# Weight panels of a transformer stack: a ring of two raw panels and four low parts becomes one ring of six, written in place

## What is computed

```python
for l in range(2):                          # D = 1024, SEQ = 256
    mod = silu(c) @ w_mod[l] + b_mod[l]     # [1, 6*D]: shift1, scale1, gate1, shift2, scale2, gate2
    h = rms_norm(x, norm1) * (1 + scale1) + shift1
    proj = h @ w_in                         # pooled part u, queries, keys/values of 3 branches, gates
    mix = concat([pool_mixer(u), nsa_mixer(q, k, v, gates)]) @ w_out
    x = x + gate1 * mix
    h2 = rms_norm(x, norm2) * (1 + scale2) + shift2
    x = x + gate2 * (square(relu(h2 @ w_ff1)) @ w_ff2)      # D_FF = 4096
# then one layer: projections, dilated attention, a two-way SSD scan, gated mix, layer norm,
# a feed-forward of width 4096, layer norm
```

## Time and profile before

| | before |
|---|---|
| median of 3 runs | 1370.56 us (1369.36 to 1371.61) |
| the profiled execution | 1369.93 us, its span 1368.1 us |
| TensorE matmul busy | 1270.2 us (93%) |
| VectorE busy | 937.6 us (69%) |
| ScalarE busy | 620.8 us (45%) |
| DMA moved | 247.69 MB, 49.7% of 16 engines' time on SyncE's queue |
| mean granted TensorE clock | 0.944 of full speed |

### The profile page before, as it was taken

The page is one execution under the profiler, slowest core; times in us unless marked ns, Lnnn a source line. Parts: engine busy times, 40 slices in busy tenths (PEclk is TensorE's granted clock), DMA queues, the critical chain, the costliest instruction groups (busy, mean ns, idle before and its releaser), DMA issues.

```text
span 1368.1 us, 21735 instructions
## 1 busy us (share of the span) xinstructions
PE 1270.2 (93%) x8834; PEld 1162.2 (85%) x8834; DVE 937.6 (69%) x1223; ACT 620.8 (45%) x828; POOL 38.4 (3%) x42
## 2 busy tenths in 40 slices
PE   6699999999998989899999998998889998999997
PEld 6587897999988779799998997886769987899996
DVE  5778868887875687775557559987865653755553
ACT  2444225444444522454444444468875532644432
POOL 1001200000000130000000000000000000000000
PEclk8699699999999989999999999999889999999999
DMA  9534554776744064465555642356744451555530
GB/s 381 214 132 154 185 199 165 281 285 242 283 155 154 31 243 156 166 216 184 184 184 215 208 154 99 120 197 205 231 159 143 155 177 60 185 196 185 186 140 31
DMA packets 43621, 247.69 MB, mean 181 GB/s; under 512 B 4160, under 2 KB 12368, under 8 KB 15520
## 3 DMA queue, kind: packets, MB, share of 16 engines
q1 hardware_dynamic: 43104, 244.57, 49.7%
q0 software_dynamic: 448, 2.14, 0.5%
HBM read 245.58 MB, written 1.11 MB: 180 GB/s over the span
## 4 chain that ended last, share of the span: by engine, by line
PE 69%; DVE 17%; DMA 6%; ACT 5%; issue 2%; SPq 0%; POOL 0%; DVEq 0%; ACTq 0%
PE bank L388 14%; PE bank L390 13%; PE bank L389 13%; PE bank L687 12%; PE bank L688 6%; DVE w_lo L383 4%; DMA arena<-in_modw 2%; DVE arena L1017 2%; ACT w_hi L378 2%; PE bank L809 2%; DVE arena L1916 1%; DVE macc L1017 1%; DMA arena<-dscr 1%; DMA raw<-in_panels 1%; PE bank L477 1%
## 5 line engine op out<-in xcount | busy, mean ns | idle before, releaser
L383 DVE TENSOR_TENSOR w_lo<-raw,w_hi 128x2048 fp32r<-128x2048 f32 x170 | 388.7, 2290 | 186.3 <-ACT w_hi L378 185.9
L378 ACT ACTIVATE w_hi<-raw 128x2048 fp32r<-128x2048 f32 x170 | 324.1, 1910 | 229.7 <-PE bank L390 117.3
L687 PE MATMUL bank<-act,w_hi 128*128 128x512 f32 x768 | 280.2, 406 | 12.3 <-DVE act L1038 5.5
L388 PE MATMUL bank<-act,w_hi 128*128 128x256 f32 x800 | 238.1, 298 | 8.6 <-DVE act L1038 7.2
L388 PE MATMUL bank<-ff_hi,w_hi 128*128 128x256 f32 (+1 forms) x816 | 230.3, 282 | 1.8 <-issue 1.0
L389 PE MATMUL bank<-act,w_hi 128*128 128x256 f32 x800 | 230.7, 288 | 0.0
L390 PE MATMUL bank<-ff_hi,w_lo 128*128 128x256 f32 (+1 forms) x816 | 230.7, 283 | 0.0
L389 PE MATMUL bank<-ff_lo,w_hi 128*128 128x256 f32 (+1 forms) x816 | 230.6, 283 | 0.0
L390 PE MATMUL bank<-act,w_lo 128*128 128x256 f32 x800 | 230.5, 288 | 0.0
L688 PE MATMUL bank<-act,w_lo 128*128 128x256 f32 x768 | 217.7, 283 | 0.0
L687 PEld LDWEIGHTS bank<-act,w_hi 128*128 128x128 f32 x768 | 146.1, 190 | 51.4 <-issue 10.9
(11 more groups left out here) (320 smaller groups left out, 1767.0 us busy)
## 6 DMA issues: line engine op xcount, KB each, us to landing
raw<-in_panels SPq DMA_DIRECT2D x170, 1024.0 KB, 4.9
arena<-in_modw SPq DMA_DIRECT2D x48, 1024.0 KB, 6.8
mixf<-dscr SPq DMA_DIRECT2D x8, 512.0 KB, 6.0
arena<-dscr SPq DMA_DIRECT2D x8, 512.0 KB, 4.9
mixf<-dscr SPq DMA_DIRECT2D x8, 256.0 KB, 6.3
arena<-dscr SPq DMA_DIRECT2D x8, 256.0 KB, 6.4
cst<-in_cst SPq DMA_DIRECT2D x1, 1251.5 KB, 7.6
arena<-in_x SPq DMA_DIRECT2D x1, 1024.0 KB, 5.0
```

The source lines that it names most:

```text
L378: nc.scalar.activation(w_hi[slot(k)][:, :], raw[:, k % RAW, :], ACT.Copy).then_inc(hi_done, 1)
L383: nc.vector.tensor_tensor(w_lo[slot(k)][:, :], raw[:, k % RAW, :], w_hi[slot(k)][:, :].bitcast(F32), ALU.subtract).then_inc(lo_done, 1)
L388: nc.tensor.matmul(o, wh, xh, start=start, stop=False, skip_group_check=skip)
L687: nc.tensor.matmul(bank[4 + c][:, :], wh[:, s:s + P], act2[:, kc, :, :], start=kc == 0, stop=False)
```

## The change

`raw` and `w_lo` become one ring of six panels. The low part overwrites the raw panel that it is made from. `load` of panel n waits until TensorE has used panel n-6; the first six loads wait for nothing. The memory is the same. The four high parts stay as they are, with their waits.

SyncE's order changes with it. Panels 2 to 5 are loaded at the start, and every later load stands earlier in the order in relation to the units and fetches around it: in the first two layers load 14 now stands ahead of unit 17, load 15 ahead of unit 18, load 16 ahead of unit 19, load 17 ahead of units 20 and 21. In the feed-forward of layer 0 each pass has load, unit, load, unit, load, load. In the third layer the list is load 22, 23, fetches, 24, 25, fetches, 26 and so on, as before, without the loops around it.

Since six slots and four panels in a pass don't divide, the loops of six passes become two passes with three bodies each, on SyncE, ScalarE, VectorE and TensorE.

```diff
-        raw = sb("raw", [P, RAW, PANEL])
+        with nc.sbuf_tensor("raw", [P, RING_W, PANEL], F32) as raw:
+            pass
+        ring_w = sb("ring_w", [P, RING_W, PANEL], F32R)
         w_hi = [sb(f"w_hi{i}", [P, PANEL], F32R) for i in range(SPLIT)]
-        w_lo = [sb(f"w_lo{i}", [P, PANEL], F32R) for i in range(SPLIT)]
...
+        def place(m, k):
+
+            return divmod(4 * (m.c if isinstance(m, Turn) else m) + k, RING_W)
...
+        def landed(eng, m, k):
+            n, at_slot = place(m, k)
+            eng.wait_ge(raw_ready[at_slot], 16 * (n + 1) + (32 * m.i if isinstance(m, Turn) else 0))
...
         def load(sp, m, k):
 
-            sp.wait_ge(lo_done, 4 * m + k - RAW + 1)
-            sp.dma_start(raw[:, k % RAW, :], a["panels"][4 * m + k]).then_inc(raw_ready[k % RAW], 16)
+            n, at_slot = place(m, k)
+            if n:
+                sp.wait_ge(split_free, SPLIT + 4 * m + k - RING_W + 1)
+            sp.dma_start(w_raw(m, k), a["panels"][4 * m + k]).then_inc(raw_ready[at_slot], 16)
...
             m = 11 * l
-            load(sp, m, 2)
-            load(sp, m, 3)
             if l == 0:
                 load_mod(sp, l, 8)
-            if l == 0:
                 load_mod(sp, l, 9)
-            for k in (4, 5, 6):
-                load(sp, m, k)
+            load(sp, m, 6)
+            load(sp, m, 7)
             if l == 0:
                 load_mod(sp, l, 10)
-            load(sp, m, 7)
             load(sp, m, 8)
+            load(sp, m, 9)
             if l == 0:
                 load_mod(sp, l, 11)
-            for k in (9, 10, 11):
-                load(sp, m, k)
+            load(sp, m, 10)
             load_mod(sp, l, 12)
+            load(sp, m, 11)
             load_mod(sp, l, 13)
+            load(sp, m, 12)
             load_mod(sp, l, 14)
-            load(sp, m, 12)
             load_mod(sp, l, 15)
             load(sp, m, 13)
-            for u in (16, 17, 18):
-                load_mod(sp, l, u)
+            load_mod(sp, l, 16)
             load(sp, m, 14)
+            load_mod(sp, l, 17)
+            load(sp, m, 15)
+            load_mod(sp, l, 18)
+            load(sp, m, 16)
             load_mod(sp, l, 19)
-            load(sp, m, 15)
+            load(sp, m, 17)
             load_mod(sp, l, 20)
             load_mod(sp, l, 21)
-            for k in (16, 17, 18):
+            for k in (18, 19, 20, 21):
                 load(sp, m, k)
-            with sp.Fori(1, FF_STEPS // 2 - 1) as i:
-                load(sp, m + i, 15)
...
+            with sp.Fori(0, FF_PASSES) as i:
+                for n in range(1, 4):
+                    mm = Turn(i, m + n)
+                    load(sp, mm, 18)
                     for mp in range(2):
-                        sp.wait_ge(mod_used, MOD_PANELS * l + 20 + 2 * i + mp + 1)
-                        sp.dma_start(modw[:, mp, :], a["modw"][MOD_PANELS * l + 20 + 2 * i + mp]).then_inc(modraw[mp], 16)
-                for k in (16, 17, 18):
-                    load(sp, m + i, k)
+                        if ahead:
+
+                            u = MOD_PANELS * l + 20 + 2 * n + mp + 6 * i
+                            sp.wait_ge(mod_used, u + 1)
+                            sp.dma_start(modw[:, mp, :], a["modw"][u]).then_inc(modraw[mp], 16)
+                        load(sp, mm, 19 + mp)
+                    load(sp, mm, 21)
             e = m + FF_STEPS // 2 - 1
-            load(sp, e, 15)
             for u in (34, 35) if ahead else (22, 23):
                 load_mod(sp, l, u)
-            load(sp, e, 16)
-            load(sp, e, 17)
+            for k in (18, 19, 20, 21):
+                load(sp, e, k)
...
             dve.wait_ge(hi_done, 4 * m + k + 1)
-            nc.vector.tensor_tensor(w_lo[slot(k)][:, :], raw[:, k % RAW, :], w_hi[slot(k)][:, :].bitcast(F32),
+            nc.vector.tensor_tensor(w_lo(m, k), w_raw(m, k), w_hi[slot(k)][:, :].bitcast(F32),
                                     ALU.subtract).then_inc(lo_done, 1)
...
+            for k in range(2, RING_W):
+                load(sp, 0, k)
             for l in range(layers):
                 sp_layer(sp, l, l + 1 < layers)
```

More of the change, by code:

```diff
@@ L176, in build @@
         act_ready = sem("act_ready")
-        raw_ready = [sem(f"raw_ready{i}") for i in range(RAW)]
+        raw_ready = [sem(f"raw_ready{i}") for i in range(RING_W)]
         hi_done = sem("hi_done")
@@ L296, in slot, with __init__, __rmul__, w_raw @@
             return k % SPLIT
+        class Turn:
+            def __init__(self, i, c):
+                self.i, self.c = i, c
+            def __rmul__(self, four):
+                return 3 * four * self.i + four * self.c
+        def place(m, k):
+            return divmod(4 * (m.c if isinstance(m, Turn) else m) + k, RING_W)
+        def w_raw(m, k):
+            return raw[:, place(m, k)[1], :]
+        def w_lo(m, k):
+            return ring_w[:, place(m, k)[1], :]
+        def landed(eng, m, k):
+            n, at_slot = place(m, k)
+            eng.wait_ge(raw_ready[at_slot], 16 * (n + 1) + (32 * m.i if isinstance(m, Turn) else 0))
         RING = "ADAD" + "DDAD" + "D" * 5 + "A" * 8 + "D" * 7 + "A" * 8
@@ L524, in cmp @@
                     s = slice(jj * P, (jj + 1) * P)
-                    last = mm3(bank[6][:, 0:60], w_hi[slot(L_CMP)][:, s], w_lo[slot(L_CMP)][:, s], tbh[:, jj, :], tbl[:, jj, :],
+                    last = mm3(bank[6][:, 0:60], w_hi[slot(L_CMP)][:, s], w_lo(m, L_CMP)[:, s], tbh[:, jj, :], tbl[:, jj, :],
                                jj == 0, jj == 15)
@@ L705, in pe_ff @@
                 pe_mod(pe, 12 * l + 10, macc, MOD_AT + 40)
[L706 to L712, removed]
+            with pe.Fori(0, FF_PASSES) as i:
+                for n in range(1, 4):
+                    mm, j = Turn(i, m + n), j0 + 2 * n + 6 * i
+                    up(mm, k0 + 1, j + 1, 1)
+                    down(mm, k0 + 2, j, 0, False, False)
+                    up(mm, k0 + 3, j + 2, 0)
+                    down(mm, k0 + 4, j + 1, 1, False, False)
+                    if mods == "ahead":
+                        pe_mod(pe, 12 * l + 10 + n + 3 * i, macc, MOD_AT + 40 + 4 * n + 12 * i)
             e = m + FF_STEPS // 2 - 1
@@ L991, in ff_schedule @@
             step(m, j0 + 1, k0 + 1, 1, None, (k0 + 5, k0 + 6), 1)
-            with eng.Fori(1, FF_STEPS // 2 - 1) as i:
-                step(m + i, j0 + 2 * i, k0 - 1, 0, k0 - 2, (k0 + 3, k0 + 4), i)
-                step(m + i, j0 + 2 * i + 1, k0 + 1, 1, k0, (k0 + 5, k0 + 6), i)
+            with eng.Fori(0, FF_PASSES) as i:
+                for n in range(1, 4):
+                    mm, j = Turn(i, m + n), j0 + 2 * n + 6 * i
+                    step(mm, j, k0 - 1, 0, k0 - 2, (k0 + 3, k0 + 4), 3 * i + n)
+                    step(mm, j + 1, k0 + 1, 1, k0, (k0 + 5, k0 + 6), 3 * i + n)
             e = m + FF_STEPS // 2 - 1
@@ L1413, in finish @@
         def finish(sp):
-            for k in range(2, 6):
+            for k in range(6, 22):
                 load(sp, M2, k)
-            with sp.Fori(0, 4) as i:
-                for k in (6, 7, 8, 9):
-                    load(sp, M2 + i, k)
             load(sp, M2, 22)
@@ L1438, in finish @@
                         fetch(sp, e)
-            with sp.Fori(7, 19) as i:
-                for k in (6, 7, 8, 9):
-                    load(sp, M2 + i, k)
+            for k in range(34, 82):
+                load(sp, M2, k)
             for half in range(2):
@@ L2098, in _ @@
                 if u in (5, 6):
-                    sp.dma_start(raw[:, u - 5, :], a["panels"][u - 5]).then_inc(raw_ready[u - 5], 16)
+                    load(sp, 0, u - 5)
+            for k in range(2, RING_W):
+                load(sp, 0, k)
             for l in range(layers):
```

20 lines of the change are left out of this document (10 added, 10 removed).

## The result

| | before | after |
|---|---|---|
| median of 4 runs each | 1369.96 us (1365.85 to 1371.61) | 1404.01 us (1400.38 to 1409.16) |
| the profiled execution | 1369.93 us | 1405.27 us, its span 1403.4 us |
| TensorE matmul busy | 1270.2 us | 1281.4 us |
| mean granted TensorE clock | 0.944 | 0.935 |

The ratio is 1.0256, 95% interval 1.0215 to 1.0297: slower by 34 us. The forecast was 1394.0 in a range up to 1404, so the direction was right, the size was short by 10 us, and the median lies just outside. Four more runs of the changed kernel, with a second profile, gave 1398.11 (1395.32 to 1404.27). Every run lists its mean granted clock, and the time goes with it: the two shortest of the eight (1395.32 and 1395.45 us) had 0.941, the longest (1409.16) 0.929.

The account below looks back on a forecast made before the run. TensorE's matmuls bound the kernel, busy 93% of the span, about 98 us idle. From 1369.93 us, gains of 14.2 and losses of 37.9 (21.4 + 8.4 + 6.3 + 1.8) gave 1393.6, stated as 1394, range 1380 to 1404.

Parts of the forecast that it names:

- the last units: Last w_mod units of the first two layers: late by 1 to 3 us, costing +0.6 and +1.2 us.
- End of the attention, +21.4: Layers 0 and 1: units 17 and 19, queued behind waiting loads, land late; +10.9 and +10.5 us, before clock loss.
- The clock: TensorE's clock drops after the holes before mod(4) and the sums: 1.8 + 2.4 us per layer, +8.4, between 0 and 12.
- unit 12: Layer 1: this unit is issued behind a load whose awaited panel is long released, winning 1.0 us.
- Feed-forward of layer 0, +6.9: One late unit costs 1.05 us in each of six passes, +6.3 (0 to 9); the layer's last units add +0.6.
- Gains, -14.2: Panel 2 gaps 8.8, unit 12 of layer 1 1.0, first down projection of layer 3 0.9, scan 3.5 us.
- The gaps at panel 2: First two layers: earlier panel 4 wins 1.7 us in layer 0, 4.7 plus 2.4 of clock in layer 1; sum -8.8.
- The scan: Loads leave right behind the previous fetches, shortening three waits in TensorE's path: -3.5 us, between 0 and -7.
- rival A: Faster: the units' late issue is hidden and only the earlier panels count, 1355.7 us; chance 0.04.
- Costs put at 0: Split in place costs nothing; longer loop bodies taken as 0, with up to 2 us for instruction fetch.
- Rival B: Slower by the two holes alone: no clock lost at them, loop absorbs its late unit, 1378.9 us; chance 0.13.
- Rival C: Slower still: loop loses 1.5 us a pass, clock 12, gains 9, longer bodies cost 2; 1407 us; chance 0.08.

Follow-up runs that it names:

- Experiments 1: Changed kernel with the w_mod units at the end of the attention of layers 0 and 1 again ahead of the loads: 1368.45 us, 0.9984 of before.
- 4: Kernel before, with SyncE waiting ahead of load 14, unit 18 and unit 19 until panels 8, 9 and 10 are used: 1407.31 us, 1.0266 of before.
- 5: Changed kernel with only unit 17 moved ahead of load 14 in the first two layers: 1389.48 us.
- 6: Changed kernel with only unit 19 moved ahead of load 16 in the first two layers: 1382.03 us.
- 9: Kernel before with only the feed-forward loops of the first two layers unrolled to two passes of three bodies: 1369.26 us, ratio 1.000.
- 10: Kernel before with 17 idle matmuls (2.0 us) ahead of the second half of panel 5 of layer 1: 1369.85 us.
- experiment 2: Changed kernel with feed-forward units issued a pass early, behind loads that have gone some 6 us earlier: 1392.34 us, 1.0162 of before.

## Why the prediction was right or wrong

**The mechanism** was right at each place where a loss was forecast: unit 17 behind panel 8, unit 19 behind panel 10, one unit in each loop pass, the last units. Experiments 1, 4, 5 and 6 show it from both sides.

**End of the attention, +21.4, with clock +29.8.** The traces have +33.0: TensorE is busy 10.5 us longer (8.4 forecast for the clock) and idle 22.5 longer (21.4). Unit 17 landed 8.7 us behind the release of panel 8, not 7.4, and a whole 8.32 behind its own issue, so TensorE stood 4.50 us before mod(4), not 3.2; unit 19 landed 7.3 behind panel 10, as said. The Trainium skill, DMA: Bandwidth & Descriptors, section Bandwidth, gives 6.15 us for 1 MB, measured on transfers issued from GpSimd. Here SyncE issues them, and the changed kernel's panels landed in 4.8 at the median and its units in 6.9, so the trace agrees with it for neither.

**The clock.** At the holes it was lost as forecast, if by 2 us more: low for 17.1 us in layer 0 and 13.7 and 20.5 in layer 1, never before. The step that failed is that it was looked for only there (8.4 us in the sum, 12 at the upper end) and put at nothing where the change brings no wait. In the attention of layer 1 the same work ran 5.3 and 10.0 us slower in the two profiles. In the eight profiles with the ring and no idle work, or with it ahead of panel 50, the stretch averages 50.2 us, 4.5 over before. Together with 1.0 for unit 12, 3.2 more at the holes, 1.7 more at the last units and in the third layer, 1.1 of other gains that didn't come, 1.3 less in the attention of layer 0, 0.9 less in its feed-forward and 0.6 less at panel 50, that makes 8.7 us: 1402.3, beside 1401.8 for the median of eight runs. In the kernel before this stretch sat at its fast case in both profiles, which the prediction had no way to see from one of them.

The whole execution says the same. The clock was low for 152 us of it before and 185 after (means of two profiles). A stretch at half the clock can lose half its length, so an upper estimate of what the 32 us more cost is 16 us, where the forecast's clock terms come to 6.0 (8.4 lost, 2.4 won back at panel 2). The two runs of the changed kernel with the least low clock (0.941) took 1395.4 us, 2 us over the forecast. Together this puts the miss on the clock; why it is low in those stretches stays open.

**Feed-forward of layer 0, +6.9.** The traces have +6.0; the six passes of the loop, each losing 0.9 to 1.6 us, lost 6.8 and 6.4 in the two profiles (6.3 forecast), and the start of the feed-forward took a little less; undoing it alone saved 9.5 us with the tail of layer 1 (1401.8 to 1392.3), 8.9 on top of the other edit.

**Gains, -14.2.** The gaps at panel 2 gave -1.6 and -6.6 (forecast -1.7 and -7.1). The scan gave 2.5 for 3.5, but in part by luck: the waits for fetches did get shorter, yet TensorE's idle time did not, and three kernels without the ring (4, 9 and 10) took 63.1, 63.5 and 64.9 us there when the clock was low for 13.7 us of it and not for 20.5. The down projection gave 1.2 for 0.9. Unit 12 gave 0 for 1.0: the prediction took a wait of VectorE for time of TensorE. With both losses taken away the kernel stood 10.6 us under before. That is 3.9 us over the time of rival A (1355.7), and in line with the rule behind it, which the Trainium skill gives in DMA: Bandwidth & Descriptors, Rules for kernel authors: issue early, wait late. The trace agrees with the rule for the panels; the change had broken it for the units in the same queue.

**Costs put at 0**: the split in place (2289 ns for 2290) and the longer loops (ratio 1.000) were 0. Rival B is out, since the clock was lost at the holes. Rival C came near the right time by the wrong way: the passes lost 1.1 us each and not 1.5, the longer bodies 0 and not 2, and the gains were 12.1 and not 9. Of its 12 us for the clock at the holes, 10.5 were found.

## What to carry to other kernels

SyncE's queue issues in order, so a wait added to one transfer is a wait added to all behind it: unit 17 left 0.37 us behind the load that had waited for panel 8. When a buffer ring gets deeper and its loads get a later condition, list what stands behind each load, when its slot is free and when it is needed, and put it ahead of any load whose condition comes later than that; here that turned +2.1 to +2.6% into -0.8% with the same buffers. In a loop, issue a transfer that the next pass needs behind loads whose condition has already come; experiment 2 did this, and the pass went back to 23.6 us. And where a kernel's clock is low for a tenth of its time, allow for a shift of those stretches in the range of the forecast, also where the change brings no wait.

## What the hardware showed that was not expected

The same 242 matmuls took from 45.6 to 55.7 us, with 17.1 to 37.5 us of low clock among them, and the slower cases have no wait for a transfer that the fastest lacks. And 2.0 us of idle matmuls ahead of panel 50 cost the kernel before nothing that can be told from noise (1369.85 for 1369.13, ratio 1.0001, 0.9986 to 1.0016): the part they stood in front of ran at 1.00 throughout and took 2.6 us less, where it had a low stretch of 3.4 us before. The same idle matmuls inside panel 51 cost 3.9 us (ratio 1.0028).
